# Conv tiles, idle products, unrolled expert pairs and a phased gather in a two-layer hybrid decoder step

## What is computed

```
for l in range(2):
    hn   = rmsnorm(h, norm_mix[l])
    proj = hn @ w_in[l]                    # 1024 -> 3592: q f i og z xbc dt
    conv = silu(conv_b + sum(conv_w[tap] * xpad[tap:]))   # 4 taps over x|B|C
    h    = h + concat(hgrn2(q, f, i, og), ssd(conv, z, dt)) @ w_out[l]
    hn   = rmsnorm(h, norm_ffn[l])
    h    = h + (swiglu(hn) if l == 0 else top2_of_8_experts(hn))
y = rmsnorm(h, norm_final)
```

## Time and profile before

| | us |
|---|---|
| median of 3 runs | 1856.56 (1852.85 to 1860.59) |
| profiled execution: its own time | 1851.54 |
| its span | 1849.7 |
| PE busy | 1767.4 (96%) |
| DVE busy | 1294.1 (70%) |
| ACT busy | 1036.2 (56%) |
| mean granted TensorE clock | 0.963 |

### The profile page before, as it was taken

How to read it: one execution, slowest core, us unless ns; L and a number is a source line. 1 busy time by engine, 2 the same in 40 slices (tenths; PEclk the granted TensorE clock), 3 DMA queues, 4 the chain that set the end, 5 groups by cost and what they waited for, 6 DMA issues and landing times.

```text
span 1849.7 us, 24674 instructions
## 1 busy us (share of the span) xinstructions
PE 1767.4 (96%) x9550; PEld 1538.5 (83%) x9550; DVE 1294.1 (70%) x1099; ACT 1036.2 (56%) x936; POOL 108.6 (6%) x101
## 2 busy tenths in 40 slices
PE   7999998999999998997999999999999999999997
PEld 7987888999989988885888877888778888788886
DVE  5636455444346355546988888888888888888897
ACT  4443223333333352226777777777777777777776
POOL 2002130000000011210400000000000000000200
PEclk8998889999999988788999999999999999999999
DMA  9349134443453412135999999999989999999995
GB/s 305 126 159 270 35 98 152 149 155 103 139 176 114 154 47 53 45 97 197 374 397 394 394 362 332 393 370 398 374 307 395 373 386 393 319 392 380 380 383 190
DMA packets 272637, 474.41 MB, mean 256 GB/s; under 512 B 41578, under 2 KB 103266, under 8 KB 272504
## 3 DMA queue, kind: packets, MB, share of 16 engines
q1 hardware_dynamic: 266432, 452.50, 68.6%
q10 hardware_dynamic: 3368, 12.75, 2.1%
q0 software_dynamic: 2704, 7.39, 1.4%
HBM read 454.82 MB, written 29.84 MB: 262 GB/s over the span
## 4 chain that ended last, share of the span: by engine, by line
PE 87%; DVE 7%; ACT 3%; issue 2%; DMA 0%; DVEq 0%; ACTq 0%; SPq 0%
PE ps L1642 16%; PE ps L1643 16%; PE ps L2234 11%; PE ps L1637 8%; PE ps L1638 8%; PE ps L2255 6%; PE ps L2134 3%; PE ps L1832 3%; PE ps L1722 3%; PE ps L1817 2%; DVE cvt L1158 2%; PE ps L2273 1%; PE ps L2152 1%; PE ps L1870 1%; PE ps L2097 1%
## 5 line engine op out<-in xcount | busy, mean ns | idle before, releaser
L1523 DVE TENSOR_TENSOR spL<-ring,spH 128x2048 fp32r<-128x2048 f32 x336 | 765.0, 2294 | 120.6 <-ACT spH L937 119.4
L937 ACT ACTIVATE spH<-ring 128x2048 fp32r<-128x2048 f32 x336 | 642.6, 1916 | 121.3 <-PE ps L2234 60.4
L1642 PE MATMUL ps<-spH,XH 128*128 128x512 f32 x896 | 357.1, 399 | 4.3 <-ACT spH L937 2.9
L1643 PE MATMUL ps<-spH,XL 128*128 128x512 f32 x896 | 352.1, 393 | 0.0
L1637 PE MATMUL ps<-hnH,spH 128*128 128x320 f32 x928 | 281.2, 317 | 18.9 <-DVE hnL L1034 10.8
L1019 DVE TENSOR_TENSOR spL<-ring,spH 128x2048 fp32r<-128x2048 f32 (+1 forms) x74 | 158.4, 2145 | 193.6 <-ACT spH L650 193.4
L1638 PE MATMUL ps<-hnL,spH 128*128 128x320 f32 x928 | 278.9, 315 | 0.0
L2234 PE MATMUL ps<-spL,XH 128*128 128x512 f32 x896 | 242.0, 392 | 4.4 <-DVE spL L1523 4.4
L650 ACT ACTIVATE spH<-ring 128x2048 fp32r<-128x2048 f32 (+1 forms) x74 | 132.8, 1800 | 200.6 <-PE ps L2134 75.3
L1642 PEld LDWEIGHTS ps<-spH,XH 128*128 128x128 f32 x896 | 168.9, 188 | 42.5 <-ACT spH L937 3.7
L2234 PEld LDWEIGHTS ps<-spL,XH 128*128 128x128 f32 x896 | 168.0, 188 | 43.2 <-DVE spL L1523 5.7
(11 more groups left out here) (348 smaller groups left out, 1910.8 us busy)
## 6 DMA issues: line engine op xcount, KB each, us to landing
ring<-in_w_exp_in_dram SPq DMA_DIRECT2D x224, 1024.0 KB, 9.2
ring<-in_w_exp_out_dram SPq DMA_DIRECT2D x112, 1024.0 KB, 9.2
ring<-in_w_in_dram SPq DMA_DIRECT2D x28, 1024.0 KB, 5.4
ring<-in_w_ffn_in_dram SPq DMA_DIRECT2D x22, 1024.0 KB, 5.1
token_rows<-token_rows ACTq DMA_DIRECT2D x1, 11776.0 KB, 41.3
ring<-in_w_ffn_out_dram SPq DMA_DIRECT2D x16, 704.0 KB, 4.6
ring<-in_w_out_dram SPq DMA_DIRECT2D x8, 1024.0 KB, 5.0
out_dram<-ring SPq DMA_DIRECT2D x32, 256.0 KB, 2.6
```

The source lines that it names most:

```text
L937: A(esplit(j)[0], src, ACT.Copy).then_inc(S("hi_done"), 1)
L1523: V.tensor_tensor(lo, eslot(j)[0], hi.bitcast(F32), ALU.subtract).then_inc(S("split_done"), 1)
L1642: mm(out, x[0], w, start=start, stop=False)
L1643: return mm(out, x[1], w, start=False, stop=False)
```

## The change

- Conv stage, both layers: a unit's high and low parts now stand between two pairs of conv tiles, and the copy-out of a chunk comes ahead of them.
- Products whose result nobody reads are added on PE: 4 in float32 of 256 columns twice at the start (`hold_early`), and 14 of 512 columns behind the sums of squares of the dense feed-forward norm and of layer 1's first norm (`hold`).
- `sel` is made ahead of `hkL`; the gather is in phases by what its operands wait for, 8 tiles with a place each, and ACT and DVE take tile by tile. The third `expert_hi` and the exponential come behind the gather.
- `places` and `gates` are cut into five pieces that DVE does after units 5, 8, 11, 14 and 17 of the first pair.
- The three looped pairs are written out in straight code; ACT's SiLU table is loaded once in the first pair and once in the last.
- `turn_rows` is in two parts around the next down unit, in banks 2, 3, 5 and again 2; tiles 6 and 7 wait for `XL` of tiles 0 and 1.

```diff
...
-FILL_AT = TAKE_AT[-1] + 2
-GATH_FIRST = (2, 3, 6, 7)
-GATH_NEXT = (2, 3, 0, 1)
+GATH_FIRST = (2, 3, 6, 7, 4, 2, 3, 6)
+GATH_NEXT = (2, 3, 5, 2)
+STEPS_AT = [5, 8, 11, 14, 17]
+def first_place(k):
+    return GATH_FIRST[k], 0
+def next_place(k):
+    return GATH_NEXT[k // 2], k % 2 * 2 * CAP
 TURN_AT = [EXPERT_UNITS.index(("up", c + 1, 1)) for c in range(EC - 1)] + [EXPERT_UNITS.index(("down", EC - 2, 0))]
...
-            with sp.Fori(0, NE // 2 - 1) as e:
+            for e in range(NE // 2 - 1):
...
+                def conv_out(k):
+                    act.wait_ge(S("conv_sum"), 8 * l + k + 1)
+                    A(cvT[:, k, 0:NPR], cvt[:, k % 2, 0:NPR], ACT.Silu)
+                    A(cvT[:, k, NPR:TOK].rearrange("p (b r) -> p b r", b=NSQ),
+                      cvt[:, k % 2, 3 + NPR:PADC].rearrange("p (b r) -> p b r", b=NSQ)[:, :, 0:LSQ],
+                      ACT.Silu).then_inc(S("conv_done"), 1)
                 for c in range(7):
...
-                    if c < C_I:
+                    if c < C_I and c not in (C_BC, C_Q):
                         split_hi(u + 2 * c + 2)
+                    if c < C_I and c not in (C_XS, C_BC):
                         split_hi(u + 2 * c + 3)
...
+                        split_hi(u + 2 * c + 3)
+                        conv_out(4 * c)
+                        conv_out(4 * c + 1)
+                        split_hi(u + 2 * c + 4)
+                        conv_out(4 * c + 2)
+                        conv_out(4 * c + 3)
...
-            act.wait_ge(S("routed"), 3)
-            A(sml[:, 9, :, 0:1], sml[:, 8, :, 0:1], ACT.Exp).then_inc(S("rt_exp"), 1)
...
-            def pair_act(it, last=False):
-                tables(SILU)
+            def gathered(it, place, ks, both=2):
+                for k in ks:
+                    bank, o = place(k)
+                    act.wait_ge(S("gath_mm"), it * 8 + (k // both * both + both))
+                    A(XH[:, k], ps[:, bank, o:o + 2 * P], ACT.Copy, scale=vec[:, 1, 8 + k:9 + k]).then_inc(S("X_done"), 1)
+            def pair_act(it, last=False, load=True):
...
                     if j == EU + UP_LAST[-1] and not last:
-                        gathered(it + 1, GATH_NEXT)
-            for j in range(AHEAD):
-                if j == AHEAD - 1:
-                    act.wait_ge(S("tkL_done"), 3)
-                expert_hi(0, j)
+                        gathered(it + 1, next_place, range(4))
+                    if j == EU + UP_LAST[-1] + 1 and not last:
+                        gathered(it + 1, next_place, range(4, KT))
+            expert_hi(0, 0)
+            expert_hi(0, 1)
+            gathered(0, first_place, range(KT), 1)
+            act.wait_ge(S("routed"), 3)
+            A(sml[:, 9, :, 0:1], sml[:, 8, :, 0:1], ACT.Exp).then_inc(S("rt_exp"), 1)
+            expert_hi(0, 2)
...
-            gathered(0, GATH_FIRST)
-            with act.Fori(0, NE // 2 - 1) as e:
-                pair_act(e)
+            for e in range(NE // 2 - 1):
+                pair_act(e, load=e == 0)
...
+                def conv_in(k):
+                    w = PADC - TAPS + 1
+                    if k >= 2:
+                        dve.wait_ge(S("conv_done"), 8 * l + k - 1)
+                    own(V.tensor_scalar(cvt[:, k % 2, 0:w], xbc[:, k, 0:w], vec[:, l, 24 + k:25 + k],
+                                        vec[:, l, 16 + k:17 + k], ALU.mult, ALU.add))
+                    for tap in range(1, TAPS):
+                        i = V.scalar_tensor_tensor(
+                            out=cvt[:, k % 2, 0:w], in0=xbc[:, k, tap:tap + w],
+                            scalar=vec[:, l, 24 + 8 * tap + k:25 + 8 * tap + k],
+                            in1=cvt[:, k % 2, 0:w], op0=ALU.mult, op1=ALU.add)
+                        if tap < TAPS - 1:
+                            own(i)
+                        else:
+                            i.then_inc(S("conv_sum"), 1)
...
+                        conv_in(4 * c)
+                        conv_in(4 * c + 1)
+                        split_lo(u + 2 * c + 3)
+                        conv_in(4 * c + 2)
+                        conv_in(4 * c + 3)
+                        split_lo(u + 2 * c + 4)
...
+            row_steps = (expert_of, round_of, row_of, gates, last_gates)
+            dve.wait_ge(S("routed"), 2)
+            dve.wait_ge(S("rank_mm"), 1)
...
+            one_hot(rank)
             dve.wait_ge(S("rstd_done"), 4)
...
+                    if first and j in STEPS_AT:
+                        row_steps[STEPS_AT.index(j)]()
                     if j == EU + UP_LAST[-1] and not last:
-                        gathered_lo(it + 1, GATH_NEXT)
+                        gathered_lo(it + 1, next_place, range(4))
+                    if j == EU + UP_LAST[-1] + 1 and not last:
+                        gathered_lo(it + 1, next_place, range(4, KT))
...
             count_rounds()
+            gathered_lo(0, first_place, range(4), 1)
             expert_lo(0, 0)
-            gathered_lo(0, GATH_FIRST)
+            gathered_lo(0, first_place, range(4, KT), 1)
             expert_lo(0, 1)
             expert_lo(0, 2)
-            places()
-            gates()
...
-            with dve.Fori(0, NE // 2 - 1) as e:
-                pair_dve(e)
+            for e in range(NE // 2 - 1):
+                pair_dve(e, first=e == 0)
...
+            def hold(n, bank):
+                for _ in range(n):
+                    mm(ps[:, bank, :], tabR[:, 0:P], tabR[:, 0:512], start=True, stop=True)
+            def hold_early(n):
+                pe.wait_ge(S("xT_done"), 1)
+                for _ in range(n):
+                    mm(ps[:, X_BANKS[0], 0:2 * P], onesf, tab[:, 0:2 * P], start=True, stop=True)
...
@@ -1679,6 +1724,7 @@
                                                 xin[0:n, t, (4 * half + k) * P:(4 * half + k + 1) * P],
                                                 ident[0:n, 0:n])
                     m.then_inc(S("xin_tr"), 1)
+            hold_early(4)
             for l in range(DEPTH):
...
             for t, (o, n) in enumerate(TILES):
                 m = mm(ps[:, 4, o:o + n], onesf[0:n], xdg[0:n, t, 0:n], start=True, stop=True)
             m.then_inc(S("ss_mm"), 1)
+            hold_early(4)
...
                 if l:
                     norm_mm(2 * l, sq)
+                    hold(14, 7)
                 def turn_small():
...
                 if l == 0:
                     norm_mm(1, sq)
+                    hold(14, 7)
                     for j in range(11):
...
-            pe.wait_ge(S("tk_done"), 9)
-            pe.wait_ge(S("tkL_done"), 3)
             def gather():
                 pe.wait_ge(S("sel_done"), 1)
...
+                outs = []
+                for k in range(KT):
+                    bank, o = first_place(k)
+                    outs.append((ps[:, bank, o:o + 2 * P], slice(k * P, (k + 1) * P)))
+                pe.wait_ge(S("tk_done"), 8)
+                for out, d in outs[:4]:
+                    mm(out, hkH[:, 0, d], sel[:, 0], start=True, stop=False)
+                    mm(out, hkH[:, 1, d], sel[:, 1], start=False, stop=False)
+                for t in range(2):
+                    pe.wait_ge(S("tkL_done"), t + 1)
+                    for out, d in outs[:4]:
+                        mm(out, hkL[:, t, d], sel[:, t], start=False, stop=False)
+                pe.wait_ge(S("tk_done"), 9)
+                pe.wait_ge(S("tkL_done"), 3)
+                for out, d in outs[:4]:
+                    mm(out, hkH[:, 2, d], sel[:, 2], start=False, stop=True).then_inc(S("gath_mm"), 1)
+                for k in range(4, KT):
+                    if k > 4:
+                        pe.wait_ge(S("XL_done"), k - 4)
+                    out, d = outs[k]
+                    for t in range(3):
+                        m = mm(out, hkH[:, t, d], sel[:, t], start=t == 0, stop=t == 2)
+                        if t < 2:
                             mm(out, hkL[:, t, d], sel[:, t], start=False, stop=False)
-                        m = mm(out, hkH[:, 2, d], sel[:, 2], start=False, stop=True)
                     m.then_inc(S("gath_mm"), 1)
-            def turn_rows(it):
...
+            def turn_rows(it, part):
+                if part == 0:
+                    pe.wait_ge(S("Xg_in"), it * 16 + 16)
+                    pe.wait_ge(S("eh_done"), it * (2 * EC) + 2 * EC)
+                for k in range(4 * part, 4 * part + 4):
+                    if k == 6:
+                        pe.wait_ge(S("XL_done"), it * 8 + (8 + 2))
+                    bank, o = next_place(k)
+                    for x in range(2):
+                        m = nc.tensor.transpose(ps[:, bank, o + x * P:o + (x + 1) * P], Xg[:, x, k * P:(k + 1) * P], ident)
                     m.then_inc(S("gath_mm"), 1)
             def scatter(t, q):
...
                             kk = 4 * (i % 2) + k
-                            if u < 2 and k % 2 == 0:
-                                pe.wait_ge(S("XL_done"), it * 4 + (kk // 2 + 1))
```

(5 more changed lines are left out.)

104 lines of the change are left out of this document (32 added, 72 removed).

## The result

The changed kernel takes a median of 1833.89 us (1826.03 to 1842.72, 10 runs) against 1857.9 us (1849.68 to 1862.6, 10 runs) for the kernel before, measured together. The ratio is 0.9878 with a 95% interval of 0.9854 to 0.9901: 22.7 us less (18.4 to 27.1). Forecast were 1829.7 us and 25.0 us less; the time lies inside the range of 1820 to 1841.

The account below looks back on a forecast made before the run. PE was taken as the bound, busy 96% of the span, with gains only from its idle or half-clock time. Terms summed to -25.0 us, giving 1829.7 us from a middle of 1854.7; range 1820.0 to 1841.0.

Parts of the forecast that it names:

- A: Start of the kernel: unread products on PE hold the clock, so low products start earlier; -3.1 us, bounds -3.4 and +0.6.
- B: Conv tiles in the two projections: reordering removes PE's waits of 4.1 and 2.7 us for ACT's high parts; -6.8 us.
- C: Two later norms: fourteen unread products fill PE's idle time and keep full clock; -3.2 us, bounds 0 and -3.5.
- D: Routing and first expert units: earlier `sel` and gather, small steps moved away; -8.0 us, bounds -8.2 and -4.0.
- E: Expert pair boundaries: straight code removes PE's waits at the first two; -3.9 us, bounds 0 and -4.5.
- The third boundary stays: Third pair boundary: PE's 0.94 us wait lies at the branch over the `If` and remains; 0 us change.
- F: Rows turned in two parts: the `sg` wait goes, a 1.3 to 1.4 us wait on `XL` replaces it; 0 us.
- G: Small steps spread over the first pair: DVE catches up between groups; 0 us, bound above +4.3.
- the weight stream: Rival in the experts: the 11.9 us gained there is given back as waits on DMA; 1841.6 us, chance 0.06.
- refill: Rival in the straight-code pairs: 28 instruction packets fetched while running each stop PE; up to 1914 us, chance 0.04.
- the products did hold the clock: Denies a rival at start and norms: added products don't raise the clock and delay real ones; 1836.6 us, chance 0.14.
- the run of small steps: First pair: bound and rival that the spread groups each stall PE, +4.3 us for all; 1834.0 us, chance 0.08.

## Why the prediction was right, and where it was off

- The sum was right: 25.0 forecast, 22.7 measured (18.4 to 27.1). Its parts were not all, and errors of both signs cancelled.
- **A** was over-sized: -3.1, measured -1.8 between the profiles, and on average 0.9 or 2.3 by the profile without products that it is held against. The step that failed is that the first four products stand while PE waits anyway. That needs the full clock; in seven of eleven profiles the clock had not yet risen, they took 3.78 us (the prediction had 3.7 as the price at half clock) and in the changed kernel's profile pushed the sums of squares from 12.24 to 13.50 and the first product to 17.62. Where they took 1.99 the low products came at 20.2 to 21.4, around the forecast's 20.9.
- **B** held: the longest wait went, no low part was late. It had priced the waits (6.8) and missed 1.3 us in layer 0, which I put down to the moved copy (not tried alone); measured are 7.7.
- **C** held, 3.1 against 3.2, though undone it was only 0.6 + 1.3.
- **D** held: 8.7 against 8.0, the clock behind the wait included. The first gather product came 2.61 us behind the ranks, as laid out.
- **E** was forecast at -3.9; it is 0 between the two profiles and -6.0 + 2.9 = -3.1 by the average of the third boundary, the sum of two errors. At the first two boundaries 6.0 us went, not 3.9: the row of waits showed 1.52 and 1.34, and I allowed 0.5 each for smaller gaps where 1.6 each lay in the units around them. That the branch and the table load stood behind these waits together is not contradicted; their shares are open. "The third boundary stays" failed: the branch cost 1.2 us before and 0.9 to 8.0 since. The Trainium skill (Runtime: NRT & Kernel Launch, section Instruction fetch mechanics) had pointed at the branch, and without it the wait was gone (8.27 us); that it was a fetch that PE stood for, no run shows; but I kept the price of one execution, 0.94, where bounds of 0 and the 3.02 us of ACT's issue stood in the same rows.
- **F** and **G** held: the wait on `XL` came, 1.09 instead of 1.3, and PE waited for no low part in the first pair beyond 0.2 us. That the order on DVE decides it, the variant with `XL` first shows.
- The rivals: the weight stream did not bind (no wait of PE on DMA in the experts, and 362 to 397 GB/s in 19 of the 20 slices that the experts fill in the page, over the 358 of the Trainium skill's page DMA: Bandwidth & Descriptors, section Where 436 GB/s comes from), refill did not come (no issue gap inside the pairs; the variant without the branch shows none at any boundary), the products did hold the clock. The instruction queue fetched less than before, 78 packets against 83. Two bounds of the rivals were mis-added: the run of small steps from 866.70 to 871.19 is 4.5 us, not 4.3, and 28 packets at 1.2 us leave 1863.3, still short of the 1865.8 of "slower". The outcome hangs on neither.
- Not foreseen was the line of the recurrences: with one and the same code there their two stretches vary by 12.0 and 14.4 us over eleven profiles, more than any single step was worth. Over all fourteen profiles the length of a stretch follows the time that its clock is 0.50, 30.7 to 71.7 us: with each us of that goes 0.38 us of length in layer 0 and 0.44 in layer 1 (correlation 0.98 both times).

## What to carry over

A branch over a large body that is never entered cost PE 1 to 8 us here, at a place where PE otherwise never stops; price it from several profiles, and look for a place where PE waits anyway (not tried here). Sum a change over stretches between the same instructions, and leave out those it doesn't touch; two whole spans differed here by 14.6 us where the change was worth 22.7. A product that nobody reads pays for certain only if it fits into the wait at half clock too, or where the clock is seen to be up ahead of it, as in the two norms. A window row's clock ahead of the first change that the trace records is not a reading; take it from the length of known instructions.

## What was not expected

- Times follow the mean granted clock: the ten runs of the changed kernel go from 1842.72 us at 0.959 to 1826.03 at 0.969. The falls lie in the recurrences and in other places each time, at 134 to 150 us in one profile, behind waits of only 1.4 and 1.8 us.
- The same four products took 1.99 or 3.78 us at 9 to 10 us, by whether the clock had risen ahead of them or at 13.4 to 14.7 us. What sets the time of the rise is open.
- One branch can stop PE twice, the second time five products on. What decides on the second stop is open too. The branch of a loop over a pair stopped PE for 1.8 to 1.9 us behind a straight first pair and for 0.2 in the kernel before; that is open as well.
